# Router of a diffusion step: ten tiles resident, turned before they are scaled, and the choice made over two halves side by side

## What is computed

```python
h = modulate(rms_norm(y, norm_ffn), m[3], m[4])            # y: (n, 2048), latent and context apart
logits = einsum('bnd,de->ben', h, w_router)                # 16 experts
aff = softmax(logits, axis=1)                              # over the experts
g, idx = lax.top_k(aff, cap)                               # cap = 2 * n // 16: 128 of 1024, 32 of 256
xs = x[idx]
hcur = silu(xs @ w_gate[e]) * (xs @ w_up[e])               # 2048 x 1024 each, per expert
ys = (hcur @ w_down[e]) * g                                # 1024 x 2048
y = y + m[5] * scatter_add(ys, idx)
```

## Time and profile before

| | us |
|---|---|
| three runs: median (lowest to highest) | 4257.04 (4248.58 to 4257.21) |
| the profiled execution, its own time | 4244.02 |
| its span, first to last instruction | 4242.5 |
| PE busy in the span | 3876.5 (91%) |
| DVE busy | 2548.1 (60%) |
| ACT busy | 1812.8 (43%) |
| POOL busy | 491.7 (12%) |

### The profile page before, as it was taken

The page is one execution under the profiler, slowest core; times in us unless marked ns, Lnnn a source line. Parts: engine busy times, 40 slices in busy tenths (PEclk is TensorE's granted clock), DMA queues, the critical chain, the costliest instruction groups (busy, mean ns, idle before and its releaser), DMA issues. The chain is left out here.

```text
span 4242.5 us, 68814 instructions
## 1 busy us (share of the span) xinstructions
PE 3876.5 (91%) x25048; PEld 3401.9 (80%) x25048; DVE 2548.1 (60%) x4837; ACT 1812.8 (43%) x2845; POOL 491.7 (12%) x453
## 2 busy tenths in 40 slices
PE   7999999999799999897986299999999999999992
PEld 3688888888688888897985288888888888888881
DVE  4645545545476766322322777777777777777774
ACT  3611111111466666110104266666666666666653
POOL 0000000000444543000000000000000000000000
PEclk9999999999799999999998599999999999999996
DMA  9433443343545463735414277778777887778776
GB/s 351 147 129 129 133 139 129 122 137 129 167 122 186 134 189 99 260 103 190 139 62 185 87 244 254 254 253 258 254 253 259 262 262 256 254 256 262 253 240 240
DMA packets 572373, 825.37 MB, mean 195 GB/s; under 512 B 23728, under 2 KB 458368, under 8 KB 560512
## 3 DMA queue, kind: packets, MB, share of 16 engines
q1 hardware_dynamic: 548448, 700.96, 50.6%
q0 software_dynamic: 23840, 123.26, 8.9%
HBM read 717.21 MB, written 108.00 MB: 195 GB/s over the span
## 5 line engine op out<-in xcount | busy, mean ns | idle before, releaser
L1831 DVE TENSOR_TENSOR e_wlo<-e_raw,e_whi 128x1024 fp32r<-128x1024 f32 x768 | 905.0, 1219 | 348.0 <-ACT e_whi L1747 345.0
L1972 PE MATMUL ps<-e_xs,e_whi 128*128 128x320 f32 x4096 | 1060.7, 345 | 16.7 <-DVE e_xs L1839 9.0
L1972 PE MATMUL ps<-e_xs,e_wlo 128*128 128x160 f32 x4096 | 935.0, 238 | 0.0
L1747 ACT ACTIVATE e_whi<-e_raw 128x1024 fp32r<-128x1024 f32 x768 | 768.9, 1054 | 384.3 <-DMA e_raw<-in_w_gate 156.4
L1972 PEld LDWEIGHTS ps<-e_xs,e_whi 128*128 128x128 f32 x4096 | 754.9, 188 | 25.2 <-DVE e_wlo L1831 12.6
L1972 PEld LDWEIGHTS ps<-e_xs,e_wlo 128*128 128x128 f32 x4096 | 770.8, 191 | 0.7
L1990 PE MATMUL ps<-e_whi,e_h 128*128 128x512 f32 x1024 | 406.1, 397 | 6.8 <-DVE e_h L1865 6.8
L1338 PE MATMUL ps<-o_whi,mhi 128*128 128x256 f32 x1280 | 364.3, 285 | 36.4 <-DMA mlo<-mixlo 33.1
L485 PE MATMUL ps<-hhi,p_whi 128*128 128x512 f32 (+1 forms) x1536 | 386.3, 360 | 8.4 <-DVE p_wlo L424 8.4
L442 DVE SCALAR_TENSOR_TENSOR p_acc<-p_modraw,cT,p_acc 128x256 f32<-128x256 f32 x960 | 386.4, 478 | 0.7 <-DMA p_modraw<-in_w_mod 0.7
L485 PE MATMUL ps<-hlo,p_whi 128*128 128x512 f32 (+1 forms) x1536 | 383.3, 358 | 0.0
(11 more groups left out here) (237 smaller groups left out, 5766.5 us busy)
## 6 DMA issues: line engine op xcount, KB each, us to landing
e_raw<-in_w_gate SPq DMA_DIRECT2D x64, 2048.0 KB, 8.2
e_raw<-in_w_up SPq DMA_DIRECT2D x64, 2048.0 KB
e_raw<-in_w_down SPq DMA_DIRECT2D x64, 2048.0 KB, 7.9
p_modraw<-in_w_mod SPq DMA_DIRECT2D x128, 512.0 KB, 3.7
m_raw<-in_w_mod SPq DMA_DIRECT2D x16, 2048.0 KB, 14.7
p_raw<-in_w_in SPq DMA_DIRECT2D x64, 512.0 KB, 4.8
o_raw<-in_w_out SPq DMA_DIRECT2D x16, 2048.0 KB, 8.9
projT<-p_out_st POOLq DMA_DIRECT2D x32, 640.0 KB, 3.3
```

Source lines behind the costliest of these rows:

```text
L1747: nc.scalar.activation(piece(whi, c, q), piece(raw, c, q), ACT.Copy).then_inc(w_hi_made, 1)
L1831: nc.vector.tensor_tensor(piece(wlo, c, q), piece(raw, c, q), piece(whi, c, q).bitcast(F32), ALU.subtract).then_inc(w_lo_made, 1)
L1972: last = nc.tensor.matmul(bank[:, 0:cols], w[:, s, at:at + P], xs[:, k, 0:cols], start=(k == 0 and w is whi), stop=(k == KD - 1 and w is whi))
```

## The change

- `yt` holds all ten tiles; SP loads each as soon as a semaphore allows, without a wait on stores. Each tile is turned as it comes, unscaled, and the logits are made from the unscaled tile. The inverse roots of all tokens multiply the logits afterwards, in one instruction. The scaled tiles are still stored for the experts: tiles 0 to 4 are scaled by DVE between later tiles, tiles 5 to 9 by ACT after the exponentials.
- The copies of the turned tile are shared: banks 0 and 1 by ACT (`front`), banks 2 and 3 by DVE (`back`).
- In the logits' product the turned tile is stationary (128 x 128) and the 16 columns of `wrm` move. The result has tokens on partitions, so that the transposes of L1505 go. The shift is made as a row on all partitions by 32 products with a broadcast stationary operand.
- The affinities go into `byhalf`, so that one tile of 96 partitions holds the latent tokens 0 to 511, the latent tokens 512 to 1023 and the context, each for 16 experts. Sixteen rounds over 96 x 512 take the place of 4 over 16 x 256 and 16 over 16 x 1024. The two sorted lists of 128 are then merged: one is reversed, and in each place the larger of the two is kept, with its number.
- The first two chunks of the experts' weights are loaded by SP in the router's block, behind the tiles, and `gate_row` is made there by PE and ACT, behind the turning of the affinities.
- In attention, POOL's subtraction for `kll` is issued as four over 128 x 448.

```diff
+        KPARTS = 4
...
-                nc.gpsimd.tensor_tensor(kll[:, h, :], kraw[:], khh[:, h, :].bitcast(F32), ALU.subtract
-                                        ).then_inc(k_lo_made, 1)
+                for n in range(KPARTS):
+                    f = slice(n * (KCOL // KPARTS), (n + 1) * (KCOL // KPARTS))
+                    last = nc.gpsimd.tensor_tensor(kll[:, h, f], kraw[:, f], khh[:, h, f].bitcast(F32), ALU.subtract)
+                last.then_inc(k_lo_made, 1)
...
             for t in range(NT):
-                if t >= 2:
-                    sp.wait_ge(xn_stored[t % 2], 16 * (t // 2))
-                    sp.wait_ge(y_turned, 4 * (t - 1))
-                sp.dma_start(yt[:, t % 2, :], y_d[t * P:t * P + P, :]).then_inc(y_in[t % 2], 16)
+                if t >= FT:
+                    sp.wait_ge(y_in[t - FT], 16)
+                sp.dma_start(yt[:, t, :], y_d[t * P:t * P + P, :]).then_inc(y_in[t % FT], 16)
+            for c, name in enumerate(("w_gate", "w_up")):
+                sp.dma_start(raw[:, c, :].rearrange("p (k n) -> p k n", k=KD),
+                             v[name][0:1, :, 0:CW].rearrange("a (k p) n -> p (a k) n", p=P)
+                             ).then_inc(w_loaded[c], 16)
...
+            for t in range(NT):
+                square(t)
+                front(t)
+                if t == FT:
+                    roots(0)
+            roots(1)
+            act.wait_ge(soft_step, 4)
+            nc.scalar.activation(soft[:], soft[:], ACT.Exp).then_inc(soft_step, 1)
+            act.wait_ge(rms_step, 6)
+            for t in range(FT, NT):
+                act.wait_ge(y_turned, 4 * t + 4)
+                nc.scalar.activation(yt[:, t, :], yt[:, t, :], ACT.Copy, scale=rinv[:, t:t + 1]).then_inc(late_scaled, 1)
...
-                    last = nc.tensor.matmul(ps[0:E, 4 + t % 2, 0:P], wrm[:, cond[t], k, :],
-                                            yT[:, t % 2, k * P:k * P + P], start=(k == 0), stop=(k == KD - 1))
+                    last = nc.tensor.matmul(lg[:, t, :], yT[:, t % 2, k * P:k * P + P], wrm[:, cond[t], k, :],
+                                            start=(k == 0), stop=(k == KD - 1))
...
+            for t in range(NT):
+                back(t)
+                if t == FT:
+                    means(0)
+                if t == FT + 1:
+                    inverses(0)
+                    scale_early(0)
+                    scale_early(1)
...
+            for r in range(CAP_L // 8):
+                at = slice(8 * r, 8 * r + 8)
+                if r:
+                    dve.wait_ge(pick_step, 3 * r)
+                nc.vector.max(top[:, at], aff[:]).then_inc(pick_step, 1)
+                dve.wait_ge(pick_step, 3 * r + 1)
+                nc.vector.max_index(place[:, at], top[:, at], aff[:]).then_inc(pick_step, 1)
+                dve.wait_ge(pick_step, 3 * r + 2)
+                nc.vector.match_replace(aff[:], top[:, at], aff[:], -1.0).then_inc(pick_step, 1)
...
+            nc.vector.tensor_tensor(first[:], top[0:E, :], topB[:], ALU.is_ge).then_inc(merge_step, 1)
+            nc.vector.tensor_tensor(topL[:], top[0:E, :], topB[:], ALU.max)
+            dve.wait_ge(merge_step, 6)
+            nc.vector.tensor_tensor(numL[:], num[0:E, :], numB[:], ALU.subtract).then_inc(merge_step, 1)
+            dve.wait_ge(merge_step, 7)
+            nc.vector.tensor_tensor(numL[:], numL[:], first[:], ALU.mult).then_inc(merge_step, 1)
+            dve.wait_ge(merge_step, 8)
+            nc.vector.tensor_tensor(numL[:], numL[:], numB[:], ALU.add).then_inc(merge_step, 1)
```

More of the change, by code:

```diff
@@ L1461, in _, with front @@
-            square(0)
-            for t in range(NT):
-                if t + 1 < NT:
-                    square(t + 1)
-                for b in range(4):
+                act.wait_ge(y_in[t % FT], 16 * (t // FT + 1))
+                if t:
+                    act.wait_ge(y_square, t)
+                nc.scalar.activation(junk[:], yt[:, t, :], ACT.Square, accum_out=sums[:, t:t + 1]).then_inc(y_square, 1)
+            def front(t):
+                for b in range(2):
                     act.wait_ge(y_turned, 4 * t + b + 1)
@@ L1474, in _ @@
         @block.tensor
         def _(pe):
-            pe.wait_ge(consts_made, 6)
-            for k in range(KD):
-                last = nc.tensor.matmul(ps[0:E, 6, 0:2], wr[:, k, :], addT[:, :, k], start=(k == 0),
-                                        stop=(k == KD - 1))
+            pe.wait_ge(consts_in, 16)
+            pe.wait_ge(consts_made, 4)
+            for c in range(2):
+                for k in range(KD):
+                    last = nc.tensor.matmul(ps[:, 7, c * E:c * E + E], addT[:, c, k:k + 1].broadcast_to([P, P]),
+                                            wr[:, k, :], start=(k == 0), stop=(k == KD - 1))
@@ new lines, in back, with means @@
+            def back(t):
+                for b in range(2, 4):
+                    dve.wait_ge(y_turned, 4 * t + b + 1)
+                    if t >= 2 and b == 2:
+                        dve.wait_ge(logits_done, t)
+                    nc.vector.tensor_copy(yT[:, t % 2, 512 * b:512 * b + 512], ps[:, b, :]).then_inc(back_read, 1)
+            def means(half):
+                f = slice(half * FT, half * FT + FT)
+                dve.wait_ge(y_square, half * FT + FT)
+                nc.vector.tensor_scalar(mean[:, f], sums[:, f], 1.0 / D, EPS, ALU.mult, ALU.add).then_inc(rms_step, 1)
@@ new lines, in _ @@
+            means(1)
+            inverses(1)
+            dve.wait_ge(rms_step, 6)
+            dve.wait_ge(bank_copied, 1)
+            dve.wait_ge(logits_done, NT + 1)
+            nc.vector.tensor_tensor(soft[:], lg, rinv[:].unsqueeze(2).broadcast_to([P, NT, E]), ALU.mult
+                                    ).then_inc(soft_step, 1)
+            dve.wait_ge(soft_step, 1)
+            for c, tiles in enumerate((slice(0, LAT // P), slice(LAT // P, NT))):
+                n = tiles.stop - tiles.start
+                last = nc.vector.tensor_tensor(soft[:, tiles, :], soft[:, tiles, :],
+                                               shift[:, c:c + 1, :].broadcast_to([P, n, E]), ALU.add)
@@ L1629, in experts @@
     xs_made = sem("e_xs_made")
-    w_loaded = [sem(f"e_w_loaded{s}") for s in range(2)]
+    gate_row, raw, w_loaded = (v[n] for n in ("gate_row", "raw", "w_loaded"))
     w_hi_made = sem("e_w_hi_made")
@@ L1925, in _ @@
         def _(pe):
-            for c in range(2):
-                for b in range(4):
-                    if c:
-                        pe.wait_ge(gate_read, b + 1)
-                    for k in range(4):
-                        col = modT[:, 5 * KD + 4 * b + k, c:c + 1].broadcast_to([P, P])
-                        last = nc.tensor.matmul(ps[:, 4 + b, k * P:k * P + P], col, ident[:], start=True, stop=True)
-                    last.then_inc(gate_turned, 1)
             def turn_xs(n, groups, banks_free):
```

262 lines of the change are left out of this document (130 added, 132 removed).

## The result

The changed kernel took 4196.5 us (median of four runs, 4194.7 to 4208.0) where the kernel before took 4252.8 beside it (four runs). The ratio of the runs is 0.9881, 95% interval 0.9859 to 0.9902. That is 56 us faster by the medians and 51 by the ratio, where 87 were forecast. The forecast of 4170 is 26 us too low, and 4196.5 lies just outside the range of 4142 to 4196.

What follows compares the result with a forecast made beforehand. PE bounds the experts' block, DVE alone the router's last 62 us; in attention PE waits for DVE. Gains summing to 87.3 off 4244.0 give 4156.7, plus 13.0 for the median, 4170; range 4142 to 4196.

Steps and rivals of the forecast that it cites:

- the front: Router up to the last logits: ten tiles of 5.4 us at full clock after the shift, gain 29.5 us (21 to 34).
- Rival (c): Router's front runs at the lower clock, some 3 us more per tile: gain 57, so 4200; chance 0.08.
- The term for the shift: Start of the router's front: the shift's 64 matmul records on PE take 10.1 us (7 to 13).
- Choice: Router's selection rounds: sixteen over 512 columns at 2.29 us each, gain 31.5 us from 68.2 (30 to 33).
- rival (d): Router's choice costs by elements, not columns: 139 us more, 4309, slower than before; chance 0.03.
- Softmax: Router, between last logits and first round: 5.1 us against 6.8, gain 1.7 (1.0 to 2.4).
- merge: Router, after the choice: some seven added steps of 0.2 us, a cost of 1.4 us (1.0 to 2.5).
- Experts' start: Experts' block up to PE's first product: modulates from S + 11.2 instead of S + 17.2, gain 6.0 us.
- Attention: Split low keys let DVE in between POOL's instructions: less waiting and higher PE clock, gain some 20 us (7 to 37).
- rival (b): Attention's split buys nothing, POOL's four parts win each time: total gain 67 to 74, 4183 to 4190; chance 0.2.
- the longest cast: Sign in attention's profile after: DVE's L996 takes under 1.2 us in its longest cases, instead of 2.5.
- The median's distance: Whole kernel: the median of runs lies 13.0 us above the profiled execution, taking 4156.7 to an expected 4170.

Runs made afterwards that it cites:

- experiment 2: Changed kernel with the router's 16 columns written four times side by side, so 64 columns move in the logits' product: 4163.8 us, ratio 0.9821 to the kernel before.
- experiment 3: Changed kernel with the router's 16 columns written twice side by side, so 32 columns move in the logits' product: 4186.6 us, ratio 0.9874 to the kernel before.
- experiment 7: Changed kernel with the two first loads of the first expert's weights put back at the experts' block's start: 4207.3 us, ratio 0.9913 to the kernel before.
- experiment 4: Changed kernel with the low keys' subtraction as one instruction again, not four: 4217.1 us, ratio 0.9936 to the kernel before.
- experiment 8: Kernel before with only the low keys' subtraction in four parts, router and experts untouched: 4228.7 us, ratio 0.9978 to the kernel before.
- experiment 5: The changed kernel itself run once more, unaltered, beside the kernel before: 4197.5 us, ratio 0.9892.

## Why the prediction was right and wrong

**The step that failed** is this one, in the part on the front: "It works without a gap of more than a few tenths, so I take full clock after the shift." The first half came true, PE works without a gap, and the conclusion did not follow. The engine was busy all the time and was held at the lower clock for most of it (0.55 in the mean). The prediction took the clock from PE's pauses alone; the fall that it had read in attention came behind two waits. It did not ask what PE does when it is busy. In the old front's logits 128 columns moved, in the new one's 16, and experiments 2 and 3 show that with more of them, and nothing else changed on PE, the full clock is granted in this very stage. The Trainium skill's page "TensorE: Matmul & The Clock Gate", in its section on the clock gate (Part 1), has the rule that the prediction followed: the clock goes by how busy PE has been. By busy time as the profile gives it, 105.9 of 108.1 us, the trace does not agree, since the granted clock is 0.55, and the measurement decides.

**Rival (c)** was the right one by name, "the front runs at the lower clock, because small matmuls with weight loads don't hold it up", and got 0.08. Its argument against rested on the old front, whose logits have the other form. Its price was too low as well: 3 us a tile were said, and it is 4.7 (10.13 - 5.4) where the clock is 0.50 throughout. At the lower level not only the logits take twice the time (0.21 us a record instead of 0.11) but the transposes do too, 3.65 instead of 1.97. The ten tiles took 92.4 us (2219.15 to 2311.53) instead of 55, and the shift 3.7 more than was said: 41 us, which is the whole way from a gain of 29.5 to a loss of 11.4. That rival (c)'s 4200 came near to the 4196.5 is luck: its price was too low, and the 13 us spoken of below made up for it.

**The rest of the front's working stands.** With 64 columns the tile took 5.27 us against 5.4, no load was waited for, and the copies of ACT and DVE lay beside PE. The term for the shift (10.1, bounds 7 to 13) was mis-sized, 13.84, by the same cause: the row it was taken from rises to full clock on its way, this one stays at 0.50. With the clock restored, the profiled execution of experiment 2 took 4157.7 us, where the sum had been 4156.7. That they meet so closely is chance in part: the front still gave 2.9 us less than its term, and attention, with no long cast in that profile, 3.1 more. By the ratio the gain is 76 us.

**Choice**: 31.5 forecast, 31.3 measured, by columns as assumed; rival (d), elements, is out. **Softmax** 1.7 and 2.0, **merge** -1.4 and -2.0. **Experts' start**: 6.0 and 5.8, and experiment 7 shows it one to one.

**Attention**: at most pairs of heads the mechanism is as forecast (DVE gets in between POOL's parts, the first wait goes, PE enters the second at full clock), and such a pair gains 3.3 us (a head of 38.7 us becomes one of 35.4), where 2.7 was forecast. As a whole rival (b), that the split buys nothing, is out by experiments 4 and 8. But its mechanism, POOL winning each time, is what happens at one or two heads in six of the eight profiles (experiment 5). The prediction could have seen it: it put the 8.0 us wait down to POOL being late, but DVE's timeline of the kernel before, shown below, has an L996 of 8.80 us just ahead of it, where the prediction had 2.5 for the longest. So two of its signs failed: the longest cast is 9.23 us and not under 1.2, and the waits of the turning (now L1092) sum to 25.8 us in 15, not to some 15.

```profile
1531.92 8.80 DVE L996 CAST athi<-prT 128x128 fp32r<-128x128 f32 x1
```

The page "SBUF — State Buffer" of the Trainium skill, in its section on the two sides of SBUF, says that GpSimd and a VectorE instruction in a two-port mode or with two inputs in SBUF lock each other out for the length of a whole instruction. The trace agrees, with a cast of 2.50 us ending with POOL's in experiment 4, and one of 0.72 when POOL's is in four parts. The casts of 9.23 us are held through ten instructions, which that sentence doesn't cover. The size was 20 against 15.7 in the first profile and 16 in the mean of eight. Two more parts of it were off: the second wait grew from 1.67 to 2.41, and the L1014 of the first head was not helped at all (6.00 us; the prediction had expected 3 of its 5.60 back).

**The median's distance**: 13.0 us had been added for the difference between the profiled execution and the median. In the three later comparisons the median of the kernel before was 4252.8, 4241.1 and 4240.3, against 4257.0 at first and 4244.0 of the profiled execution. So most of these 13 were chance, and they hid part of the error: without them the forecast would have been 4157. One more slip, which moves nothing: the high bounds add to a gain of 113, not 112.

## What to carry to other kernels

Ask of a new matmul form not only what a record costs but at which clock it runs: here PE, busy 98% of the time with 128 x 128 loads and 16 moving columns, was at 1.2 GHz for most of a stage, and moving three more copies of the same columns was 38 us faster. When operands trade places, price the stage at both levels of the clock and give the lower one a real chance, unless a row shows this very form at full clock. And compare the granted clock of a stretch with PE's busy time: where over a whole stage busy is near 1 and the clock near 0.5, look for another form and not for a wait. And look at the longest instruction of a group, not at the usual one: the cast of 8.80 us stood in the trace before.

## What the runs showed of the hardware

- 16 moving columns behind loads of 128 x 128, fp32, mixed with transposes: granted clock 0.55 over 108 us. 32 columns: 0.65 over 92. 64 columns: 0.87 over 70, and 1.00 in every tile past the shift.
- At the lower level a record with its load of 128 x 128 took 0.21 us instead of 0.11. That the load sets it is argued: PEld was busy 105.8 of 108.1 us, and 32 records took 6.85 us with 16 moving columns and 6.88 us with 32 (experiment 3).
- MAX8, FIND_INDEX8 and MATCH_REPLACE8 over 96 x 512 take 0.69, 0.68 and 0.67 us. MAX8 over 16 x 1024 took 1.22 and over 16 x 256 0.42, so it went by the columns, and 96 partitions cost no more than 16.
- POOL's issues of two gathers took 2.01 and 1.81 us beside DVE's subtraction between tiles in SBUF, and 1.04 and 0.89 without it (experiment 7).
- The first gather's context rows landed in 6.0 us, and in 9.6 with 4 MB of weights on the way (experiment 7).
- Attention has heads that take 35.4, some 37, 41 or 43.4 us in executions of one kernel, with the clock between 0.95 and 0.80. Those of 40 us and more are the ones with a DVE cast of 9.2 us that ends with POOL's tenth instruction, where POOL came late to the low keys. Moving POOL's start on purpose was not tried.
